# Seven block products for both down projections, with the weight sums made by adding DMA transfers

## The chip, the cores and the metric

One core of a Trainium2 chip runs the whole program in one launch. The time is that of the device, in microseconds (us): 1117.66 us is the median of three runs of the kernel before (1117.46 to 1119.12). Tokens are 512, the model is 1024 wide, the feed-forward layer 2816.

TensorE (PE in the profile) multiplies, VectorE (DVE), ScalarE (ACT) and GpSimd (POOL) do the work around it, and SyncE (SP) issues most transfers. Each engine runs its own instruction stream in order and waits on semaphores. The 16 DMA engines serve every queue.

## What is computed

Two transformer blocks, one after the other, all in float32. The parts that the change touches are the two feed-forward layers, and the norms behind them:

```
# first block                                   # second block
h = rms_norm(x, norm_ffn_pre)                   h2 = rmsnorm(x, norm2_g)
f = (silu(h @ w_gate) * (h @ w_up)) @ w_down    gate, up = h2 @ w_gate, h2 @ w_up
x = x + rms_norm(f, norm_ffn_post)              x = x + (silu(gate) * up) @ w_down
                                                return rmsnorm(x, final_g)
```

Ahead of each stand a norm, an input projection, attention and an output projection. In the first block attention is global for eight heads and windowed for eight, in the second it is causal with forget gates, beside pooled channels.

## The kernel before

**Precision.** A float32 operand is split in two fp32r parts, `high` (a rounded copy, made by ACT) and `low` (the rest, made by DVE), and a product is three matmuls: high by high, high by low, low by high.

**Weights.** They come as chunks of 512 KB (128 partitions by 8 tiles of 128 by 128). SP's `load(c)` puts chunk `c` in `raw`, a ring of four slots, once `vec_split` has read the chunk four before. `act_split` writes `wh` once the matmuls on the chunk four before are done (semaphore `used`), `vec_split` writes `wl`.

**Gate and up.** The first four of the 22 column tiles are multiplied plainly. The other 18 (`GROUPS`) are done by seven block products each (a two by two scheme of the Strassen kind, with 7 products of half size in place of 8), 7 products of 4 tiles by 256 tokens by 3 matmuls. One such group takes two chunks. DVE forms the sums of weight blocks that it needs (`vec_sum13`, `vec_s2`, `vec_s4`). The hidden values go to `gwhole`; `act_hidden_high` and `vec_hidden_low` split all 22 tiles to `gh` and `gl`.

**Down.** `pe_down` is plain: for each of 8 output tiles, 22 tiles of the hidden width, weights stationary, 512 tokens moving, 3 matmuls. The last output tile goes in two halves of 256 tokens, so that the norm behind it can begin on the first. Outputs stand with features on partitions. A chunk lasts PE for 8 tiles, since `DOWN` cuts the 22 tiles in 8, 8 and 6. In the first block `vec_down1` and `act_down1` square and sum the outputs, and the rest of the norm lies beside the first matmuls of `pe_in`, the second block's input projection. In the second block `vec_down2` adds x, `vec_final` multiplies by the norm's factor, and the output is stored.

**GpSimd.** It works in the first attention (`gpsimd_tick`), and then has nothing until the second (`gpsimd_attention2`). It issues no transfers.

## Time and profile before

| | us |
|---|---|
| median of 3 runs | 1117.66 |
| the profiled execution, its own span | 1115.9 |
| PE busy in it | 1092.9 (98%) |
| DVE busy | 832.3 (75%) |
| ACT busy | 612.6 (55%) |
| POOL busy | 121.2 (11%) |
| DMA: mean rate | 98 GB/s |

The span is that of one execution. Matmuls are pipelined, so a row's duration is longer than the distance from one matmul to the next; that distance, between the starts of two rows, is what a matmul costs. Stages by PE's rows: first down product 448.0 to 569.9 us, second 985.9 to 1107.75 us.

### The profile page before, as it was taken

To read this page: it belongs to the slowest core of one execution; us is meant where nothing else is said; L and a number is where in the kernel's file an instruction comes from. 1 tells how busy PE (TensorE), PEld (TensorE's weight loads), DVE (VectorE), ACT (ScalarE), POOL (GpSimd) and SP (SyncE) were. 2 spreads that over 40 slices of the span, in tenths; PEclk is the share of its full clock that TensorE was granted. 3 is DMA by queue.
4 is the path that set the end of the run, shared out by engine and by line. 5 is a ranking of instruction groups with operands and counts; after the bars stand their busy time and mean duration, and the time that the engine had idled before them with its cause. 6 is when DMAs were issued, how large, how long until landed. Compare 5 with 4: busy or idle time off the path is not lost.

```text
span 1115.9 us, 18197 instructions
## 1 busy us (share of the span) xinstructions
PE 1092.9 (98%) x6848; PEld 972.0 (87%) x6848; DVE 832.3 (75%) x1425; ACT 612.6 (55%) x1109; POOL 121.2 (11%) x143
## 2 busy tenths in 40 slices
PE   9999989999999999999999999999999999999997
PEld 6788877899999999888898887787899999988886
DVE  6898886798989888833378878566699898884333
ACT  6787785486555555522255558545555555563231
POOL 1476744000000000000000004200000000000000
PEclk9999999999999999999999999999999999999999
DMA  7323312312332333333313320031233233333312
GB/s 282 126 59 93 88 49 96 113 65 87 115 98 95 113 114 112 125 105 113 110 70 115 93 81 17 20 103 65 79 114 114 97 95 113 114 132 114 95 57 76
DMA packets 34150, 109.30 MB, mean 98 GB/s; under 512 B 4368, under 2 KB 7056, under 8 KB 33936
## 3 DMA queue, kind: packets, MB, share of 16 engines
q1 hardware_dynamic: 33312, 107.22, 29.5%
q8 instruction: 55, 0.90, 0.3%
q10 hardware_dynamic: 752, 0.92, 0.3%
q14 instruction: 31, 0.25, 0.1%
HBM read 100.78 MB, written 2.10 MB: 92 GB/s over the span
## 4 chain that ended last, share of the span: by engine, by line
PE 89%; DVE 5%; ACT 3%; issue 1%; DMA 1%; POOL 1%; ACTq 0%; SPq 0%; DVEq 0%
PE bank L551 13%; PE bank L553 13%; PE bank L552 13%; PE bank L2145 11%; PE bank L2144 11%; PE bank L2143 11%; PE bank L1086 2%; PE bank L1076 2%; PE bank L1031 1%; PE bank L1032 1%; PE bank L1033 1%; PE bank L1159 1%; PE bank L1160 1%; PE bank L1161 1%; PE bank L2630 1%
## 5 line engine op out<-in xcount | busy, mean ns | idle before, releaser
L472 DVE TENSOR_TENSOR wl<-raw,wh 128x1024 fp32r<-128x1024 f32 x108 | 134.0, 1242 | 132.0 <-ACT wh L460 131.6
L460 ACT ACTIVATE wh<-raw 128x1024 fp32r<-128x1024 f32 (+1 forms) x109 | 114.0, 1049 | 163.7 <-PE bank L553 152.8
L2143 PE MATMUL bank<-h,wh 128*128 128x256 f32 x576 | 163.0, 283 | 0.0
L2144 PE MATMUL bank<-h,wh 128*128 128x256 f32 x576 | 163.0, 283 | 0.0
L2145 PE MATMUL bank<-h,wl 128*128 128x256 f32 x576 | 163.0, 283 | 0.0
L2145 PE MATMUL bank<-hh,wl 128*128 128x256 f32 x432 | 122.3, 283 | 0.0
L2144 PE MATMUL bank<-hl,wh 128*128 128x256 f32 x432 | 122.3, 283 | 0.0
L2143 PE MATMUL bank<-hh,wh 128*128 128x256 f32 x432 | 122.2, 283 | 0.0
L551 PE MATMUL bank<-gh,wh 128*128 128x512 f32 x308 | 119.8, 389 | 0.0
L552 PE MATMUL bank<-gl,wh 128*128 128x512 f32 x308 | 119.8, 389 | 0.0
L553 PE MATMUL bank<-gh,wl 128*128 128x512 f32 x308 | 119.8, 389 | 0.0
L551 PE MATMUL bank<-hh,wh 128*128 128x512 f32 x288 | 116.2, 403 | 1.8 <-DVE wl L472 1.4
L552 PE MATMUL bank<-hl,wh 128*128 128x512 f32 x288 | 112.4, 390 | 0.0
L553 PE MATMUL bank<-hh,wl 128*128 128x512 f32 x288 | 112.3, 390 | 0.0
L2143 PEld LDWEIGHTS bank<-h,wh 128*128 128x128 f32 x576 | 110.6, 192 | 0.0
L2144 PEld LDWEIGHTS bank<-h,wh 128*128 128x128 f32 x576 | 110.6, 192 | 0.0
L2145 PEld LDWEIGHTS bank<-h,wl 128*128 128x128 f32 x576 | 110.6, 192 | 0.0
L2144 PEld LDWEIGHTS bank<-hl,wh 128*128 128x128 f32 x432 | 82.9, 192 | 0.1
L2143 PEld LDWEIGHTS bank<-hh,wh 128*128 128x128 f32 x432 | 82.9, 192 | 0.1
L2145 PEld LDWEIGHTS bank<-hh,wl 128*128 128x128 f32 x432 | 82.9, 192 | 0.0
L2297 ACT ACTIVATE wh<-raw 128x512 fp32r<-128x512 f32 (+1 forms) x72 | 60.4, 844 | 40.8 <-PE bank L2145 40.6
L2505 ACT ACTIVATE ta<-ta 128x256 f32<-128x256 f32 x72 | 29.8, 414 | 89.9 <-DVE ta L2324 89.9
(309 smaller groups left out, 2652.6 us busy)
## 6 DMA issues: line engine op xcount, KB each, us to landing
raw<-weights SPq DMA_DIRECT2D x181, 512.0 KB, 3.6
xres<-x_t SPq DMA_DIRECT2D x8, 512.0 KB, 6.2
sw<-ta SPq DMA_DIRECT2D x36, 64.0 KB, 2.0
out_t<-final SPq DMA_DIRECT2D x6, 256.0 KB, 2.1
q<-sw SPq DMA_DIRECT2D x10, 128.0 KB, 2.3
q<-ta SPq DMA_DIRECT2D x10, 128.0 KB, 2.3
rope<-angles SPq DMA_DIRECT2D x1, 1024.0 KB, 10.3
sw<-ta ACTq DMA_DIRECT2D x4, 64.0 KB, 2.8
```

The costliest lines, as they stand in the source:

```text
L460: act.activation(wh[:, j, :, n], raw[:, j, :, n], ACT.Copy).then_inc(high_split, 1)
L472: v.tensor_tensor(wl[:, j, :, :], raw[:, j, :, :], wh[:, j, :, :].bitcast(F32), ALU.subtract)\
L551: pe.matmul(bank[:, :], wh[:, slot, b, :], ah[:, k, :], start=first and n == 0, stop=False)
L552: pe.matmul(bank[:, :], wh[:, slot, b, :], al[:, k, :], start=False, stop=False)
L553: ins = pe.matmul(bank[:, :], wl[:, slot, b, :], ah[:, k, :], start=False, stop=last and n == len(blocks) - 1)
L1076: ins = pe.matmul(dst, a, b, start=i == 0, stop=i == len(todo) - 1)
L1086: ins = pe.transpose(bank[:, q * P:(q + 1) * P], pr1[:, s % PR1, q, kb * P:(kb + 1) * P], ident[:, :])
L2143: pe.matmul(o, wh_half[:, h, k, :], high[:, k, :], start=first and k == 0, stop=False, skip_group_check=True)
L2144: pe.matmul(o, wh_half[:, h, k, :], low[:, k, :], start=False, stop=False, skip_group_check=True)
L2145: ins = pe.matmul(o, wl_half[:, h, k, :], high[:, k, :], start=False, stop=k == HK - 1, skip_group_check=True)
L2297: act.activation(high, src, ACT.Copy).then_inc(gu.unit_high.of, 1)
L2505: act.activation(t, t, ACT.Silu).then_inc(gu.taken.of, 1)
```

## The change

Each down product is cut in two by two blocks: hidden halves of 11 tiles (`PAIR_TILES`), output halves of 512 columns, token halves `EARLY_TOKENS` and `LATE_TOKENS` of 256. Seven block products replace eight. In a product the tokens are now stationary (two blocks of 128) and 512 weight columns move, so the result has tokens on partitions. One product takes 11 tiles by 2 token blocks by 3 matmuls, and six chunks (`PER`), the sixth half empty.

- **Weight sums.** Four of the seven products need sums of weight blocks (S1 to S4). GpSimd makes them in device memory, by 8 transfers for each layer, each 768 rows of 4 KB (3.15 MB). Four copy a block, four add one to what is there (`accum_op`). Each waits for the one before. Both layers' 16 stand behind the first attention's work.
- **Token sums.** `gpsimd_token_sums` makes the sums of hidden values for the products P5, P6, P7 and P4 in batches of 4, 4 and 3 tiles. It stands on GpSimd behind all 16 transfers. `act_token_high` and `vec_token_low` split them in the down phase, one product ahead.
- **Taking the products.** `act_take` copies a product from PSUM to `ftok`, `vec_join` adds another. The order of products is P1, P2, P6, P5, P7, P3, P4.
- **Rows and features.** In the first block the normed rows are turned back by 32 transposes on PE (`pe_turn_rows`), 16 within the last product and 16 within `pe_in`. In the second, x is turned to rows by 32 transposes (`pe_turn_x`) within P6 and P5, and the output is stored by rows.
- **Gone.** `act_hidden_high` and `vec_hidden_low` (22 each for a layer), the sums on PE behind the down phases, the 512-wide reciprocals, `vec_scale` in the first block.

```diff
+SEVEN = (P1, P2, P6, P5, P7, P3, P4)
+BASE = {P1: W11, P2: W12, P4: W22}
+SUMMED = {P5: S1, P6: S2, P7: S3, P3: S4}
...
+        STEPS_SUMMED = {S1: 2, S2: 4, S4: 6, S3: 8}
+
+        def gpsimd_weight_sums(g, dn):
+            s = [dn.sums[i].rearrange("c p k n -> (c p) (k n)") for i in range(4)]
+            row = 4 * KB
+            g.dma_start(s[S1], blocks(dn, W21), max_dma_last_dim=row).then_inc(dn.sums_made, 16)
+            g.wait_ge(dn.sums_made, 16)
+            g.dma_start(s[S1], blocks(dn, W22), accum_op=ALU.add, max_dma_last_dim=row).then_inc(dn.sums_made, 16)
+            g.wait_ge(dn.sums_made, 32)
+            g.dma_start(s[S2], s[S1], max_dma_last_dim=row).then_inc(dn.sums_made, 16)
...
+        def gpsimd_token_sums(g, dn):
+            gu, sums, n = dn.gu, dn.token_sums, len(BATCHES)
+            early, late = EARLY_TOKENS, LATE_TOKENS
+            for batch in BATCHES:
+                t = ktiles(0, batch)
+                hidden_made(g, gu, t.stop - 1)
+                g.tensor_tensor(gwhole[:, t, early], gwhole[:, t, late], gwhole[:, t, early], ALU.subtract).then_inc(sums.of, 1)
+            reached(g, gu.product, 2 * GROUPS)
+            for i, batch in enumerate(BATCHES):
+                reached(g, sums, i + 1)
+                g.tensor_tensor(t2_whole[:, batch, :], gwhole[:, ktiles(1, batch), early], gwhole[:, ktiles(0, batch), early], ALU.add)\
+                    .then_inc(sums.of, 1)
...
+        def pe_block(pe, dn, x, chunk, row, b):
+            p, k, slot = SEVEN[x], 2 * chunk + row, (dn.c0 + PER * x + chunk) % RING
+            bank, n = down_pair(p)[b], slice(b * P, (b + 1) * P)
+            high, low = high_tokens[x % 2][:, k, n], low_tokens[x % 2][:, k, n]
+            pe.matmul(bank[:, :], high, wh_row[:, slot, row, :], start=k == 0 and p in (P1, P2, P5), stop=False, skip_group_check=True)
+            pe.matmul(bank[:, :], high, wl_row[:, slot, row, :], start=False, stop=False, skip_group_check=True)
+            return pe.matmul(bank[:, :], low, wh_row[:, slot, row, :], start=False, stop=k == PAIR_TILES - 1, skip_group_check=True)
...
+        def act_down_step(act, dn, x, n):
+            act_split(act, dn.c0 + PER * x + RING + n)
+            if x < 6 and n < len(BATCHES):
+                act_token_high(act, dn, x + 1, n)
...
@@ block.sync: load(c) @@
+                if down_chunk(c):
+                    name, x, i = down_chunk(c)
+                    p = SEVEN[x]
+                    if p in BASE:
+                        source = w_in[STORED0[name] + PER * BASE[p] + i]
+                    else:
+                        sp.wait_ge(downs[name].sums_made, 16 * STEPS_SUMMED[SUMMED[p]])
+                        source = downs[name].sums[SUMMED[p], i]
...
@@ block.gpsimd @@
             for t in range(TICK0, TICKS):
                 gpsimd_tick(g, t)
+            gpsimd_weight_sums(g, down1)
+            gpsimd_weight_sums(g, down2)
+            gpsimd_token_sums(g, down1)
             gpsimd_attention2(g)
+            gpsimd_token_sums(g, down2)
```

POOL, before, from the end of the first attention on (`sq`, `rh`: its last sums; `pr2`: the second attention's weights):

```order
L1475 TENSOR_TENSOR rh_69<-xres_57 128x512 [waits n_groupB_added,at1_added]
L1477 TENSOR_TENSOR sq_70<-sq_70,rh_69 128x512 [waits n_groupB_added,gpsimd_link]
L1930 TENSOR_SCALAR pr2_107<-pr2_107,rden_76 128x128 [waits at2_inverted]
L1930 TENSOR_SCALAR pr2_107<-pr2_107,rden_76 128x256 [waits at2_inverted]
```

Now, at the same place (the first layer's transfers, the turn to the second's, its last, and the token sums):

```order
L1494 TENSOR_TENSOR sq_70<-sq_70,rh_69 128x512 [waits n_groupB_added,gpsimd_link]
L2504 DMA down1_weight_sums<-weights 768x1024
L2506 DMA down1_weight_sums<-weights 768x1024 [waits down1_weight_sums]
L2508 DMA down1_weight_sums<-down1_weight_sums 768x1024 [waits down1_weight_sums]
...
L2518 DMA down1_weight_sums<-weights 768x1024 [waits down1_weight_sums]
L2504 DMA down2_weight_sums<-weights 768x1024 [waits down1_weight_sums]
...
L2518 DMA down2_weight_sums<-weights 768x1024 [waits down2_weight_sums]
L2546 TENSOR_TENSOR gwhole_83<-gwhole_83 128x4x256 [waits tiles_read,down2_weight_sums]
L2546 TENSOR_TENSOR gwhole_83<-gwhole_83 128x4x256 [waits gate_up_product]
L2546 TENSOR_TENSOR gwhole_83<-gwhole_83 128x3x256 [waits gate_up_product]
L2550 TENSOR_TENSOR t2_whole_90<-gwhole_83 128x1024 [waits down_token_sums,gate_up_product]
```

What stood directly behind the attention now has 16 transfers and twelve additions ahead of it; the first addition waits for the last transfer.

ACT, before, early in the first down phase (`wh<-raw`: weight splits; `sw<-bank`: the square of an output tile):

```order
L460 ACTIVATE wh_61<-raw_60 128x1024 [waits chunks_used,weights_loaded2]
L1937 ACTIVATE sw_66<-bank3 128x512 [waits chunks_used]
L460 ACTIVATE wh_61<-raw_60 128x1024 [waits chunks_used,weights_loaded3]
L460 ACTIVATE wh_61<-raw_60 128x1024 [waits chunks_used,weights_loaded0]
```

Now, in the second product of the first down phase (`high_tokens0<-t2_whole`: the tokens of P6, the third product):

```order
L2695 ACTIVATE ftok_91<-bank6 128x2x256 [waits chunks_used]
L2695 ACTIVATE ftok_91<-bank7 128x2x256
L491 ACTIVATE wh_61<-raw_60 128x1024 [waits chunks_used,weights_loaded2]
L2570 ACTIVATE high_tokens0_86<-t2_whole_90 128x1024 [waits chunks_used,down_token_sums]
L491 ACTIVATE wh_61<-raw_60 128x512 [waits chunks_used,weights_loaded3]
L2570 ACTIVATE high_tokens0_86<-t2_whole_90 128x1024 [waits chunks_used,down_token_sums]
```

Behind each of the first weight splits stands a split of tokens, which waits for GpSimd's sums; the weight splits behind it wait too.

## Rows read from the trace of the kernel before

**Rows 1.** The page: span, then busy time of each engine, share, instructions.

```profile
PE 1092.9 (98%) x6848; PEld 972.0 (87%) x6848; DVE 832.3 (75%) x1425; ACT 612.6 (55%) x1109; POOL 121.2 (11%) x143
```

**Rows 2.** The page: the chain that ended last, its share of the span.

```profile
PE 89%; DVE 5%; ACT 3%; issue 1%; DMA 1%; POOL 1%; ACTq 0%; SPq 0%; DVEq 0%
```

**Rows 3.** Timeline, first down product: start us, us, engine, line, operation, out<-in.

```profile
448.04 0.40 PE L551 MATMUL bank<-gh,wh 128*128 128x512 f32 x1
...
552.79 0.28 PE L2628 MATMUL bank<-gh,wh 128*128 128x256 f32 x1
...
569.90 0.28 PE L1176 MATMUL bank<-hh,wh 128*128 128x256 f32 x1
```

**Rows 4.** Timeline, second down product on PE: its first and last matmul.

```profile
985.90 0.40 PE L551 MATMUL bank<-gh,wh 128*128 128x512 f32 x1
...
1107.63 0.28 PE L2630 MATMUL bank<-gh,wl 128*128 128x256 f32 x1
```

**Rows 5.** Timeline, PE: four transposes (L675) between matmuls.

```profile
604.91 0.40 PE L553 MATMUL bank<-hh,wl 128*128 128x512 f32 x1
...
605.15 0.60 PE L675 MATMUL bank<-ident,ta 128*128 128x128 f32 x4
...
605.50 0.47 PE L560 MATMUL bank<-hh,wh 128*40 128x512 f32 x1
...
605.81 0.39 PE L561 MATMUL bank<-hl,wh 128*40 128x512 f32 x1
```

**Rows 6.** Timeline, PE: the sum (L620) within the input projection.

```profile
574.10 0.28 PE L1177 MATMUL bank<-hh,wl 128*128 128x256 f32 x1
...
574.46 0.47 PE L1176 MATMUL bank<-hh,wh 128*128 128x256 f32 x1
...
574.76 0.28 PE L1177 MATMUL bank<-hh,wl 128*128 128x256 f32 x1
```

**Rows 7.** Timeline, the program's end: [idle before <-releaser].

```profile
1107.95 0.42 DVE L2667 TENSOR_TENSOR xres<-xres,bank 128x256 f32<-128x256 f32 x1 [3.25 <-PE bank L2630]
...
1109.61 0.38 ACT L1702 ACTIVATE rstd<-bank 128x256 f32<-128x256 f32 x1 [0.39 <-PE bank L620]
...
1110.47 2.77 DVE L2675 TENSOR_TENSOR final<-final,rstd 128x256 f32<-128x256 f32 x8 [2.10 <-ACT rstd L1703]
...
1111.26 2.36 SPq L2730 DMA_DIRECT2D out_t<-final  x3
```

**Rows 8.** Timeline, POOL: its last piece in the first attention, its next one.

```profile
179.82 1.30 POOL L1477 TENSOR_TENSOR sq<-sq,rh 128x512 f32<-128x512 f32 x1
...
671.28 1.26 POOL L1930 TENSOR_SCALAR pr<-pr,rden 128x128 f32<-128x128 f32 x2 [490.16 <-DVE rden L1888]
```

**Rows 9.** Busy time by stretch: length; PE, PEld, DVE, ACT, POOL; PEclk, DMA share, GB/s.

```profile
8.00:22.00 14.00, 12.67 (x55) 9.85 (x55) 12.62 (x19) 11.77 (x22) 0.58 (x1) 1.00 0.91 367
...
182.00:448.00 266.00, 264.47 (x2028) 255.32 (x2027) 235.05 (x377) 153.40 (x263) 0.00 (x0) 1.00 0.33 106
...
448.00:553.00 105.00, 105.00 (x466) 87.00 (x465) 46.61 (x52) 33.32 (x41) 0.00 (x0) 1.00 0.34 112
...
1108.00:1116.00 8.00, 0.70 (x2) 0.30 (x2) 3.14 (x9) 1.61 (x4) 0.00 (x0) 0.83 0.37 131
```

**Rows 10.** The page, DMA issues: KB each, us to landing.

```profile
raw<-weights SPq DMA_DIRECT2D x181, 512.0 KB, 3.6
```

**Rows 11.** Instructions of line L1457, POOL: ns min/median/max, first and last start.

```profile
L1457 POOL TENSOR_TENSOR tb<-tb,sw x8: 1283/1690/2417, 44.5 to 142.5; 128x512 f32<-128x512 f32 x8
```

**Rows 12.** Groups by line within 448 to 553 us: xcount | busy us, mean ns | idle.

```profile
L472 DVE TENSOR_TENSOR wl<-raw,wh 128x1024 fp32r<-128x1024 f32 x22 | 26.9, 1224 | 56.5 <-ACT wh L460 56.4
...
L460 ACT ACTIVATE wh<-raw 128x1024 fp32r<-128x1024 f32 x22 | 23.3, 1058 | 68.4 <-PE bank L553 68.4
```

**Rows 13.** Timeline, one gate and up group: a load's issue and the weight sum.

```profile
381.67 20.49 SPq L2762 DMA_DIRECT2D raw<-weights  x5
...
388.11 1.22 DVE L2229 TENSOR_TENSOR first_sums<-raw 128x1024 f32<-128x1024 f32 x1
```

More of the change, by code:

```diff
@@ new lines, in gpsimd_token_sums @@
+        def gpsimd_token_sums(g, dn):
[10 more added lines that the diff above has]
+                    .then_inc(sums.of, 1)
+            for k_half in range(2):
+                for i, batch in enumerate(BATCHES):
+                    t = ktiles(k_half, batch)
+                    reached(g, sums, n + i + 1)
+                    reached(g, dn.token_low, n * k_half + i + 1)
+                    g.tensor_tensor(gwhole[:, t, late], t2_whole[:, batch, :], gwhole[:, t, late], ALU.subtract).then_inc(sums.of, 1)
@@ new lines, in chunk_rows, with pe_chunk_ready, pe_chunk @@
+        def chunk_rows(chunk):
+            return range(1 if chunk == PER - 1 else 2)
+        def pe_chunk_ready(pe, dn, x, chunk):
+            slot_wait(pe, dn.c0 + PER * x + chunk)
+            if chunk % 2 == 0:
+                reached(pe, dn.token_low, len(BATCHES) * x + chunk // 2 + 1)
+        def pe_chunk(pe, dn, x, chunk):
+            pe_chunk_ready(pe, dn, x, chunk)
+            for row in chunk_rows(chunk):
+                for b in range(2):
+                    ins = pe_block(pe, dn, x, chunk, row, b)
+            ins.then_inc(used, 1)
@@ new lines, in pe_down1, with rows_of @@
+        def pe_down1(pe):
+            for x in range(7):
+                chain_free(pe, down1, SEVEN[x])
+                if x == 1:
+                    pe_factor(pe, down1)
+                for chunk in range(PER):
+                    if x == 6 and chunk == 3:
+                        pe_turn_rows(pe, 0, (0, 1))
+                    if x == 6 and chunk == 4:
+                        pe_turn_rows(pe, 0, (2, 3))
+                    pe_chunk(pe, down1, x, chunk)
+        def rows_of(b, d):
+            return ftok[:, 4 * (b % 2) + 2 * d:4 * (b % 2) + 2 * d + 2, b // 2, :]
@@ new lines, in act_take, with vec_join @@
+        def act_take(act, dn, p, b, d):
+            act.wait_ge(used, multiplied(dn, SEVEN.index(p) + 1, 0))
+            for i in range(2):
+                act.activation(rows_of(b + i, d), as_rows(down_pair(p)[i][:, :]), ACT.Copy).then_inc(dn.taken.of, 1)
+        def vec_join(v, dn, p, b, d):
+            v.wait_ge(used, multiplied(dn, SEVEN.index(p) + 1, 0))
+            reached(v, dn.taken, {P2: 2, P7: 6, P3: 6}[p])
+            for i in range(2):
+                o = rows_of(b + i, d)
+                v.tensor_tensor(o, o, as_rows(down_pair(p)[i][:, :]), ALU.add).then_inc(dn.joined.of, 1)
@@ L2726, in store @@
-        def store(eng, half, k, tiles):
-            n = HALVES[half]
-            eng.wait_ge(x_final, KT * half + k + tiles)
-            eng.dma_start(out[:, k:k + tiles, n], final[:, k:k + tiles, n]).then_inc(out_stored, 16)
+            vec_gain(v, 3, 0)
+            reached(v, first_block, 1)
+            vec_x(v, 2, 1, as_rows(PAIR_B[0][:, :]))
+            vec_x_mean(v, 1)
+            vec_final(v, 2)
+            v.wait_ge(used, multiplied(down2, 7, 0))
+            vec_x(v, 3, 1, as_rows(PAIR_B[1][:, :]))
@@ L2778, in _ @@
                 load(c)
-            for k in range(0, KT, 2):
-                store(sp, 0, k, 2)
-            store(sp, 1, 0, 2)
-            store(sp, 1, 4, 2)
-            store(sp, 1, 7, 1)
-            sp.wait_ge(out_stored, 16 * 9)
+            for b in range(3):
+                store(sp, b, slice(0, D), 2 * b + 2)
+            store(sp, 3, slice(D // 2, D), 7)
+            sp.wait_ge(out_stored, 16 * 5)
         @block.gpsimd
```

758 lines of the change are left out of this document (462 added, 296 removed).

## The prediction

> **What bounds the kernel now.** I read the page's busy times first: PE is busy in 98% of the span [rows 1]. Then the chain of work that ended last, to see that this is work that is waited for and not only overlapping rows: 89% of it is PE [rows 2]. Then the timeline of both down phases. The first runs from 448.04 to 569.90 us, the second from 985.90 to the end of its last matmul at 1107.75, each 121.9 us without a gap [rows 3, 4]. What takes matmuls out there shortens the program, as long as nothing new makes PE wait. Last I read GpSimd and the DMA engines, because the change gives them work: GpSimd ends its part of the first attention at 181.1 us and then has nothing until 671.3 [rows 8]; the DMA engines are 33% busy from 182 to 448 us, moving 106 GB/s [rows 9]. The measured time, 1117.66, is 1.8 us above the span of the profiled execution, 1115.9; I sum on the span's rows and add the sum to 1117.66.
>
> **Down products on PE.** Seven output tiles of 22 hidden tiles and 3 matmuls are 462 matmuls of 512 columns, from 448.04 to 552.79: 104.75 us, 0.227 each [rows 3]. The seven block products are 7 x 11 x 2 x 3 = 462 matmuls of the same shape, so 104.75 us again; that the stationary side is now tokens changes nothing in the shape. What goes is the eighth tile with its sums, 552.79 to 569.90: 17.1 us for each layer. What comes:
> - Transposes. Four take 0.35 us (605.15 to 605.50), and the matmul behind them 0.31 where others take 0.23: 0.43 for four [rows 5]. Four such sets lie in the first down phase (1.7), four in the input projection (1.7), eight in the second down phase (3.4).
> - Four matmuls of one column to turn the factor, in each phase. No row has one; between 0.1 and 0.6 us, I take 0.3.
> - In the input projection a sum goes: 0.36 and 0.30 between starts where 0.12 each is usual, 0.4 [rows 6].
>
> First layer: -17.1 + 1.7 + 0.3 + 1.7 - 0.4 = -13.8. Second: -17.1 + 3.4 + 0.3 = -13.4. The program's end now lasts 8.2 us behind the last matmul: a subtraction, square, sum, two ACT steps of 0.4, eight multiplications in 2.77, and the stores [rows 7]. Afterwards there are an addition, a square beside a multiplication, two small ACT steps, one multiplication and one store. I take -1.1, with -2.5 and +1 as ends. Together **-28.3**, so 1089.4 if nothing waits.
>
> **Splits in the down phase.** Chunks now last PE 12 x 0.227 = 2.72 us in place of 5.45. In a product's 15.0 us DVE has 5.5 weight splits of 1.22 and tokens worth 2.75 of them, 10.1 us, plus at most two additions of 0.7; ACT has 8.25 of 1.06, 8.7 us, plus two copies [rows 12]. Both fit. A slot freed by PE is needed again 8.2 us later and takes 1.06 + 1.22 plus a token split of each, 4.6. The loads need 2.9 MB in 15.0 us, 192 GB/s. That is above the 112 of this phase now, but the engines moved 367 GB/s at 0.91 share early in the program [rows 9]. I cost this at nothing; if the cover is gone, DVE's 4 us of slack in a product are what is used up first. The splits of 22 hidden tiles that go lay beside PE's work and give nothing back.
>
> **The chain of transfers.** GpSimd issues the 16 transfers one at a time, each waiting for the one before, from 181.1 us. Then come the token sums. Who waits for them is ACT, at its first split of the tokens of P6, and behind that stands the weight split of the last chunk of the second product. PE comes to that chunk at 448 + 15.0 + 5 x 2.72 = 476.6 us. From the chain's end E to that chunk there are: three additions for P5 (1024, 1024 and 768 columns; 512 take 1.29 us undisturbed, so 6.9 [rows 11]), one for P6 (2.5), ACT's token split 1.06, DVE's 1.22, and half a weight split on each, of which about 1.0 is in series: 12.7. So PE loses E - 463.9 us, if that is above zero. Later products wait no more, since GpSimd makes a batch in 2.5 us and PE takes 5.4 over it.
>
> So E decides, and no row shows a transfer from memory to memory, or one that adds. I bound them by loads. At full share the engines move 367 / 0.91 = 403 GB/s [rows 9]; 3.15 MB make one pass in 7.8 us. Beside the loads of gate and up (106 of 403) it is 7.8 / 0.74 = 10.5. What a transfer costs besides: a load of 512 KB lands in 3.6 us [rows 10], of which 1.3 are the pass, so 2.3. A copy takes one pass if its write lies wholly beside its read, two if they share what limits them. An addition has two reads and a write: two passes or three.
> - Low end, 1 and 2: (10.5 + 21.0 + 4.6) x 8 = 289 us, E about 477, loss 13.
> - High end, 2 and 3: (21.0 + 31.5 + 4.6) x 8 = 457 us of this rate. By 448, 267 are done; to 476.6, beside 192 GB/s of loads, about 21 more; then PE stands, nothing is loaded, and the remaining 169 shrink to 0.77, 130. E is 607, the loss 143.
> - Taken, 1.5 and 2.5: 46.8 x 8 = 374. 267 and 21 done by 476.6, 86 left, 66 us alone. E = 543, **the loss 79**. I take the middle, since read and write go to the same memory here, where a load writes elsewhere; no row is nearer to one end.
>
> Below the low end there is little room: all 16 in one pass would end at 386, but an addition must read twice. Behind a stand of that length PE starts again at a lower clock. Where it idles, at the program's end, the granted clock of the stretch is 0.83 in place of 1.00 [rows 9]: part of it was at the lower level. I add 2 us.
>
> Sum: 1117.66 - 28.3 + 79 + 2 = **1170.4**.
>
> The Trainium skill (DMA: Bandwidth & Descriptors, Latency and other measured facts) gives copies between HBM tensors a full rate of 214 GB/s, an estimate of 14.7 us for 3.15 MB alone, near two of my passes. With that for the copies the chain would be 33 us longer at its own rate, and the loss about 104. No row here shows it.
>
> **Rivals.**
> 1. *The chain is hidden or nearly.* The loss is under 28.3 when E is under 492, that is when a copy and an addition together take less than about 38.5 us beside loads. One pass and two passes, 36.1, do; then the time is 1102, and with a slightly better rate (E under 464) 1089. For it: 67% of the DMA share is free [rows 9], and nothing else of GpSimd waits. Against: every byte is read from and written to the memory that also feeds the loads, and each of 16 completions is waited for. Chance 0.24, of which half is at 1089.
> 2. *Copies at two passes, additions at four.* (21.0 + 42.0 + 4.6) x 8 = 541; 253 left at 476.6 become 195, E is 671, the loss 208, the time 1299. It is what a copy at half a load's rate, and an addition at half a copy's, would do. The Trainium skill (Collectives: The Full Stack, on the bandwidth ceiling) has that last ratio: adding there runs at half the rate of copying, because of two source reads. Chance 0.08.
> 3. *The transfers hold up gate and up.* A load issued at 381.67 lands 3.7 us later, and DVE adds from it at 388.11 [rows 10, 13]: 2.7 us in hand. If the chain makes a load land later than 6.4 us, each of the 18 groups grows; by 1 us each, 18 us. But then the chain starts no later and the down phase starts later, so with a late chain this is swallowed by the same wait, and with a hidden one the time is 1107. I give it 0.1, within the other cases.
> 4. *The change doesn't do what it says:* PE's count of matmuls is plain from the code, so I give this nothing.
>
> **How the numbers follow.** Late chain beyond the break-even, 1118 to 1250: 0.66, the likeliest, by itself 1120 to 1240. Rival 2: 0.08. Rival 1: 0.24. The rest, 0.02, is a chain that just eats the gain. A measurement of this kernel tells 0.2%, 2.2 us, from no change. So faster 0.24, same 0.02, slower 0.74. The range reaches from the hidden case to the high end with some of rival 3: 1089 to 1250.
>
> **What would show it.** Right: GpSimd's first token addition starts near 543 us, PE idles once, for 60 to 140 us, in the first down phase at the second product's last chunk, released through ACT's token split by GpSimd; the second down phase takes 108.5 us without a gap; DMA share above 0.9 from 181 us on. Wrong: GpSimd adds tokens before 464 us; or PE's idle time is spread over the gate and up groups; or a second gap stands in the down phases, behind loads or DVE. If the copies take much more or less than 18 us and the additions than 29, the mechanism is right and its size is not.

## The result, and the profile after

The changed kernel takes 1155.2 us (median of 4 runs, 1150.1 to 1161.7), the kernel before 1117.9 (4 runs beside them); the ratio is 1.0337, 95% interval 1.0301 to 1.0372. Forecast were 1170.4, 1089 to 1250, and slower with a chance of 0.74. The profiled execution spans 1159.9 us and is the slowest of its four, so the stages below add up to 44.0 us more than before, where the medians differ by 37.4.

The stages go from one first matmul to the next, in us, read from PE's timeline (the last one ends with the start of its last matmul); differences are of the unrounded times:

| stage | before | after | difference | forecast |
|---|---|---|---|---|
| to the first layer's group phase | 266.6 | 266.7 | 0.1 | 0 |
| groups of gate and up, first layer | 181.4 | 205.1 | +23.7 | 0 |
| first down phase | 121.9 | 137.9 | +16.0 | -15.1, +79, +2 |
| projection, attention and the rest, to the second layer's groups | 234.6 | 239.3 | +4.8 | +1.3 |
| groups, second layer | 181.4 | 184.1 | +2.6 | 0 |
| second down phase | 121.7 | 120.2 | -1.5 | -13.4 |
| end | 8.2 | 6.6 | -1.7 | -1.1 |

The page of the changed kernel, first the busy time of each engine (us, share, instructions) and the slices of the span, then the added queue (packets, MB, share of 16 engines) and the chain that ended last. It answers to [rows 1, 2]: PE is busy for 9.4 us less than before, and 93% instead of 98%; 27% of the chain is DMA.

```profile
span 1159.9 us, 18071 instructions
## 1 busy us (share of the span) xinstructions
PE 1083.5 (93%) x6648; PEld 954.5 (82%) x6648; DVE 896.8 (77%) x1428; ACT 661.9 (57%) x1177; POOL 201.2 (17%) x183
...
PE   8999999999998899938998999999999999998997
...
PEclk9999999999999999977999999999999999998999
DMA  7422317998898898944651421004223333334653
...
q0 software_dynamic: 12544, 50.33, 17.6%
...
PE 52%; DMA 27%; DVE 9%; ACT 5%; issue 4%; POOL 3%; ACTq 0%; SPq 0%; DVEq 0%; POOLq 0%
```

GpSimd's timeline of the changed kernel (start, us, engine, line, operation, [idle before <-releaser]): the transfers, cut to the first four and the last two, and the token sums behind them. Before, this engine stood idle here [rows 8]. A copy is followed by the next issue 13.8 to 18.6 us later, an addition by 23.7 to 26.6; the sixteen take 326.9 us.

```profile
181.12 0.92 POOL L2504 DMA_DIRECT2D down_weight_sums<-weights  x1
196.82 1.18 POOL L2506 DMA_DIRECT2D down_weight_sums<-weights  x1 [14.78 <-DMA down_weight_sums<-weights]
223.42 0.71 POOL L2508 DMA_DIRECT2D down_weight_sums<-down_weight_sums  x1 [25.42 <-DMA down_weight_sums<-weights]
237.67 1.14 POOL L2510 DMA_DIRECT2D down_weight_sums<-weights  x1 [13.54 <-DMA down_weight_sums<-down_weight_sums]
...
465.83 0.70 POOL L2516 DMA_DIRECT2D down_weight_sums<-weights  x1 [23.02 <-DMA down_weight_sums<-weights]
481.92 1.15 POOL L2518 DMA_DIRECT2D down_weight_sums<-weights  x1 [15.38 <-DMA down_weight_sums<-weights]
508.04 6.39 POOL L2546 TENSOR_TENSOR gwhole<-gwhole 128x1024 f32<-128x1024 f32 x3 [24.98 <-DMA down_weight_sums<-weights]
514.40 7.39 POOL L2550 TENSOR_TENSOR t_whole<-gwhole 128x1024 f32<-128x1024 f32 x3
521.76 18.07 POOL L2557 TENSOR_TENSOR gwhole<-t_whole,gwhole 128x1024 f32<-128x1024 f32 x6
```

PE's and ACT's timelines of the changed kernel, and one row of DVE's: the stall of the first down phase, the waits of the second, and one in each layer's last group (the second layer's shown). They answer to [rows 3, 4], where PE had no gap. For the wait of 3.75 us the profile names no releaser (`issue`); DVE's split of that chunk, the last row, ends at 528.98, just ahead of it.

```profile
516.76 1.06 ACT L2570 ACTIVATE high_tokens<-t_whole 128x1024 fp32r<-128x1024 f32 x1 [24.50 <-POOL t_whole L2550]
...
522.40 0.80 PE L2609 MATMUL bank<-wh,high_tokens 128*128 128x512 f32 x1 [20.54 <-DVE wl L504]
529.08 0.77 PE L2609 MATMUL bank<-wh,high_tokens 128*128 128x512 f32 x1 [3.75 <-issue]
...
1030.11 0.39 PE L2070 MATMUL bank<-hh,wh 128*128 128x256 f32 x1 [2.39 <-ACT acc L2392]
1048.83 0.50 PE L2609 MATMUL bank<-wh,high_tokens 128*128 128x512 f32 x1 [1.96 <-DVE wl L504]
1054.89 0.79 PE L2609 MATMUL bank<-wh,high_tokens 128*128 128x512 f32 x1 [2.18 <-DVE wl L504]
1061.25 0.50 PE L2609 MATMUL bank<-wh,high_tokens 128*128 128x512 f32 x1 [1.12 <-DVE wl L504]
...
525.61 3.37 DVE L504 TENSOR_TENSOR wl<-raw,wh 128x1024 fp32r<-128x1024 f32 x1
```

So there are four costs, not one: the stall, longer groups, waits for DVE's splits, and small waits from the order of ACT and DVE. In the groups it is the loads. DMA issues between 182 and 440 us, of the kernel before and then of the changed one (KB each, median us from issue to landing): a load lands 9.1 us after its issue in place of 3.6 [rows 10, 13 showed single ones], and 2.7 us were in hand.

```profile
raw<-weights SPq DMA_DIRECT2D x47, 512.0 KB, 3.6
```

```profile
down_weight_sums<-weights POOLq DMA_DIRECT2D x9, 3072.0 KB, 23.4
raw<-weights SPq DMA_DIRECT2D x43, 512.0 KB, 9.1
down_weight_sums<-down_weight_sums POOLq DMA_DIRECT2D x4, 3072.0 KB, 14.6
```

### The profile page after: what moved, and what is told of

It reads as the page before. It is cut to its first block, busy times and chain, and to the rows that moved or that the text cites. A ratio compares the mean times of both kernels' runs of the same rounds, so it can differ in the third digit from the quotient of the medians.

```text
span 1159.9 us, 18071 instructions
## 1 busy us (share of the span) xinstructions
PE 1083.5 (93%) x6648; PEld 954.5 (82%) x6648; DVE 896.8 (77%) x1428; ACT 661.9 (57%) x1177; POOL 201.2 (17%) x183
## 4 chain that ended last, share of the span: by engine, by line
PE 52%; DMA 27%; DVE 9%; ACT 5%; issue 4%; POOL 3%; ACTq 0%; SPq 0%; DVEq 0%; POOLq 0%
DMA down_weight_sums<-weights 21%; PE bank L583 6%; PE bank L584 6%; PE bank L585 6%; DMA down_weight_sums<-down_weight_sums 5%; PE bank L2072 5%; PE bank L2071 5%; PE bank L2070 5%; PE bank L2609 4%; PE bank L2611 4%; PE bank L2610 4%; DVE wl L504 3%; PE bank L1093 2%; PE bank L1103 1%; ACT wh L491 1%
## 5 line engine op out<-in xcount | busy, mean ns | idle before, releaser
L504 DVE TENSOR_TENSOR wl<-raw,wh 128x1024 fp32r<-128x1024 f32 (+1 forms) x144 | 191.1, 1334 | 76.4 <-ACT wh L491 75.0
L491 ACT ACTIVATE wh<-raw 128x1024 fp32r<-128x1024 f32 (+1 forms) x145 | 145.5, 1008 | 130.1 <-PE bank L2611 59.5
L2070 PE MATMUL bank<-h,wh 128*128 128x256 f32 x576 | 165.9, 288 | 13.1 <-ACT rh L2386 13.1
L2071 PE MATMUL bank<-h,wh 128*128 128x256 f32 x576 | 165.0, 286 | 0.0
L2609 PE MATMUL bank<-wh,high_tokens 128*128 128x512 f32 x308 | 125.1, 406 | 31.0 <-DVE wl L504 27.3
L2070 PEld LDWEIGHTS bank<-h,wh 128*128 128x128 f32 x576 | 112.3, 195 | 14.7 <-ACT rh L2386 14.7
L2610 PE MATMUL bank<-wl,high_tokens 128*128 128x512 f32 x308 | 122.8, 399 | 0.0
L2611 PE MATMUL bank<-wh,low_tokens 128*128 128x512 f32 x308 | 122.4, 398 | 0.0
L2071 PEld LDWEIGHTS bank<-h,wh 128*128 128x128 f32 x576 | 112.6, 196 | 0.0
L2609 PEld LDWEIGHTS bank<-wh,high_tokens 128*128 128x128 f32 x308 | 59.3, 193 | 46.9 <-DVE wl L504 30.7
```

Of the source, the lines that this page charges most:

```text
L491: act.activation(wh[:, j, b, n], raw[:, j, b, n], ACT.Copy).then_inc(high_split, 1)
L504: v.tensor_tensor(wl[:, j, b, :], raw[:, j, b, :], wh[:, j, b, :].bitcast(F32), ALU.subtract)\
L2070: pe.matmul(o, wh_half[:, h, k, :], high[:, k, :], start=first and k == 0, stop=False, skip_group_check=True)
L2071: pe.matmul(o, wh_half[:, h, k, :], low[:, k, :], start=False, stop=False, skip_group_check=True)
L2609: pe.matmul(bank[:, :], high, wh_row[:, slot, row, :], start=k == 0 and p in (P1, P2, P5), stop=False, skip_group_check=True)
L2610: pe.matmul(bank[:, :], high, wl_row[:, slot, row, :], start=False, stop=False, skip_group_check=True)
```

## The experiments

Theory A: the transfers cost, by their end (GpSimd's token sums wait for it) and by their traffic (loads land late). Theory B: GpSimd's token sums hold up DVE's splits. Rival C: the down phases' own loads, 192 GB/s, starve PE whatever else is done. Theory D: waits made by the order of ACT's and DVE's work, with a lower granted clock behind them. Theory E: how long a load is held up depends on the transfers' packets. Stages are named as in the table above; all of them, for every kernel:

| kernel | us | ratio to before, 95% | to groups | groups 1 | down 1 | between | groups 2 | down 2 |
|---|---|---|---|---|---|---|---|---|
| before | 1118 | | 266.6 | 181.4 | 121.9 | 234.6 | 181.4 | 121.7 |
| changed | 1155.2 | 1.034 (1.030, 1.037) | 266.7 | 205.1 | 137.9 | 239.3 | 184.1 | 120.2 |
| e1 no weight sums | 1122.9 | 1.004 (1.003, 1.006) | 266.2 | 185.6 | 117.3 | 240.9 | 185.5 | 118.9 |
| e2 second layer later | 1159.8 | 1.038 (1.036, 1.039) | 268.1 | 198.4 | 142.3 | 238.4 | 184.1 | 120.2 |
| e3 copies only | 1144.4 | 1.024 (1.022, 1.027) | 266.6 | 206.1 | 117.2 | 240.9 | 185.5 | 118.9 |
| e4 no sums at all | 1105.0 | 0.989 (0.987, 0.990) | 266.6 | 185.6 | 107.5 | 240.6 | 184.1 | 110.5 |
| e5 placed | 1147.9 | 1.026 (1.024, 1.028) | 294.0 | 184.1 | 117.2 | 240.8 | 184.1 | 120.2 |
| e6 placed, paced | 1131.2 | 1.012 (1.010, 1.013) | 292.3 | 185.3 | 107.8 | 240.9 | 185.5 | 111.5 |
| e7 placed, ordered | 1147.4 | 1.026 (1.024, 1.028) | 293.9 | 184.2 | 117.3 | 236.7 | 185.4 | 120.8 |
| e8 all three | 1124.7 | 1.007 (1.004, 1.009) | 292.0 | 184.2 | 107.5 | 236.7 | 185.4 | 111.7 |
| e9 first in the groups | 1108.2 | 0.990 (0.989, 0.992) | 268.6 | 190.7 | 109.5 | 236.7 | 181.5 | 113.6 |
| e10 packets of 1 KB | 1123.1 | 1.004 (1.002, 1.006) | 266.8 | 194.2 | 109.4 | 246.8 | 181.5 | 113.5 |
| e11 packets of 8 KB | 1121.5 | 1.001 (1.000, 1.003) | 275.9 | 196.2 | 109.5 | 236.7 | 181.5 | 113.5 |
| e12 first sums later | 1109.1 | 0.992 (0.991, 0.993) | 266.4 | 190.2 | 109.8 | 236.7 | 181.5 | 115.0 |

### e1: no weight sums

```diff
-            gpsimd_weight_sums(g, down1)
-            gpsimd_weight_sums(g, down2)
...
-                        sp.wait_ge(downs[name].sums_made, 16 * STEPS_SUMMED[SUMMED[p]])
-                        source = downs[name].sums[SUMMED[p], i]
+                        source = w_in[STORED0[name] + PER * SUMMED[p] + i]
```

> All 16 transfers are left out, with the weight sums that they make: the four sum products load blocks of w_down in their place, the same bytes in the same order, and nothing waits for sums. Theory A (the transfers' end sets GpSimd's token sums, and their traffic delays the loads of the first gate and up groups): those groups fall from 205.1 us back to 181.4, and the 20.5 us gap in the first down phase is gone. Theory B (GpSimd's token sums slow DVE's splits): the second down phase stays near 120 us and the first comes down from 137.9 to about the same 120, with DVE's 128x1024 subtractions at 2.8 to 3.4 us while GpSimd adds. A and B together: 1155.2 - 23.7 - 18 - about 3 in the input projection, some 1110 to 1113. Rival C (the down phases' own loads, 192 GB/s, are what starves them): gaps behind loads stay and the time is 1125 or more. If B is wrong and the transfers did all of it: about 1092 to 1098.

Measured 1122.9. Theory A holds: the groups lose 19.5 of their 23.7 us, and the stall is gone. But I expected 1110 to 1113: without any transfer the change still costs 5 us where it should give 28. The groups stay 4 us above 181.4, the projection 6 us, and the down phases take 117 and 119 us.

### e4: no token sums either

```diff
-            gpsimd_token_sums(g, down1)
...
-            gpsimd_token_sums(g, down2)
...
-                reached(act, dn.token_sums, len(BATCHES) * (P5, P6, P7, P4).index(p) + i + 1)
+                reached(act, dn.gu.product, 2 * GROUPS)
...
-                return t2_whole[:, batch, :]
+                return gwhole[:, ktiles(0, batch), EARLY_TOKENS]
```

> As the run without weight sums, and GpSimd's token sums are left out too: the products read unsummed tokens and the splits wait for no sum. What is left of the change is PE's order, the splits and the loads. Theory B: DVE's splits of 128x1024 take 1.22 us throughout, both down phases last 108.5 to 111 us, and the time is 18 to 24 us below that of the run without weight sums, about 1089 to 1093. Rival (the splits' order and slots make PE wait, whatever GpSimd does, or the loads do): the down phases stay near 120 us and the two runs differ by under 4 us.

The run is 17.9 us below e1, and nearly all of it lies in the down phases, which are 9.8 and 8.4 us shorter: 107.5 and 110.5 us, near the 106.8 and 108.5 of the forecast's sum. This is theory B. DVE's timeline of the second down phase in e1, beside GpSimd's nine sums (start, us, line, operation):

```profile
1000.77 3.42 DVE L504 TENSOR_TENSOR wl<-raw,wh 128x1024 fp32r<-128x1024 f32 x1
1004.11 2.87 DVE L2583 TENSOR_TENSOR low_tokens<-gwhole,high_tokens 128x1024 fp32r<-128x1024 f32 x1
1006.91 2.89 DVE L504 TENSOR_TENSOR wl<-raw,wh 128x512 fp32r<-128x512 f32 x1
```

and at the same place in e4, without them:

```profile
990.42 1.23 DVE L504 TENSOR_TENSOR wl<-raw,wh 128x1024 fp32r<-128x1024 f32 x1 [1.15 <-ACT wh L491]
991.56 1.22 DVE L2583 TENSOR_TENSOR low_tokens<-gwhole,high_tokens 128x1024 fp32r<-128x1024 f32 x1
992.70 0.69 DVE L504 TENSOR_TENSOR wl<-raw,wh 128x512 fp32r<-128x512 f32 x1
```

The half-size split takes 2.89 in place of 0.69: DVE is not slower, it waits. Rival C falls: with the same down loads and nothing else, the longest gap of PE in both down phases is 0.7 us. Its 1105.0 is still above the 1089 to 1093 that I expected, by the groups and the projection (4.1, 2.6 and 4.7 us), and by 2.7 us in the down phases that no run explains. The first part is theory D's, and here it can be read. Stretches of e4's first layer, around the wait of 2.39 us at 447.7 us (length; PE, PEld, DVE, ACT, POOL; granted clock, DMA share, GB/s):

```profile
440.00:448.00 8.00, 5.61 (x46) 5.41 (x45) 5.18 (x9) 5.80 (x10) 0.00 (x0) 0.99 0.40 131
448.00:456.00 8.00, 8.00 (x41) 7.35 (x41) 6.88 (x10) 3.63 (x5) 0.00 (x0) 0.80 0.36 100
```

Behind a stand of 2.4 us the granted clock of the next 8 us is 0.80, part of it at the lower level: 1.6 us more. In the second layer of the same execution the same wait has 1.00 behind it, and that phase is 1.5 us shorter (184.1 against 185.6). So the clock's part comes in some executions and not in others.

### e2: the second layer's transfers behind the token sums

```diff
-            gpsimd_weight_sums(g, down2)
             gpsimd_token_sums(g, down1)
+            gpsimd_weight_sums(g, down2)
```

> The complete kernel; the second layer's eight transfers come behind the first down phase's token sums in place of ahead of them. Theory A: the first chain ends near 345 us, GpSimd's first token sum stands near 448 or earlier, no gap of 20 us in the first down phase. The gate and up groups run beside transfers for 164 of their 267 us only, so their excess of 23.7 us falls to about 14. The second chain then runs from about 480 to 660 us, beside the down loads, the input projection and the start of the second attention. If only waiting for the chain's end costs: 1155.2 - 18 - 9 = 1128. If its traffic delays the down loads (192 GB/s) as it delays those of the groups, the first down phase keeps 5 to 15 us of it: 1133 to 1143. Rival C (loads starve the down phase whatever the order): no shorter than 1150.

Measured 1159.8, no gain, where theory A gave 1128 to 1143. It fits the 1150 or more of rival C, which e4 rules out. The stall did go, and the groups fell by 6.7 us, as theory A says. But the eight transfers that were moved now run beside the down loads, and there they cost 25.0 us (142.3 against 117.3), where I had allowed 5 to 15. Between 495 and 600 us the DMA share is 0.98, a load lands in 10.3 us, and PE stands eight times for 1.1 to 2.7 us. The loads of e1 between 480 and 585 us land in 4.1. First e2, then e1:

```profile
raw<-down_weight_sums SPq DMA_DIRECT2D x20, 512.0 KB, 10.3
raw<-weights SPq DMA_DIRECT2D x9, 512.0 KB, 7.9
```

```profile
raw<-weights SPq DMA_DIRECT2D x33, 512.0 KB, 4.1
```

### e3: copies in place of additions

```diff
-            g.dma_start(s[S1], blocks(dn, W22), accum_op=ALU.add, max_dma_last_dim=row).then_inc(dn.sums_made, 16)
+            g.dma_start(s[S1], blocks(dn, W22), max_dma_last_dim=row).then_inc(dn.sums_made, 16)
```

(and so for the other three additions of a layer)

> The eight adding transfers copy in place of adding, so what they leave out is the additions; their number, order and waits stay. In the trace of the changed kernel a copy is waited for 13 to 18 us, an addition 22.6 to 25.4. If an addition costs its second read, the 16 take 16 x 14 to 17 = 225 to 270 us, end at 410 to 450 us, GpSimd's token sums start by 450 and the 20.5 us gap goes. The first gate and up groups: if it is any traffic at a share of 0.9 that delays the loads (theory A), they stay near 200 us, since copies fill the same window; if it is adding itself, with the engines held longer for each packet, they fall to 190 or below. Time 1127 to 1142.

The sixteen copies end at 428 us, 15.4 us each. The first down phase then takes 117.2 us, the same as without any transfer: a chain that ends ahead of the group phase's end does not stall PE, and the 20.5 us were its end and nothing else. The groups stay at 206.1: any traffic at this share delays the loads (8.6 us to landing), adding or not. 1144.4 lies 2 us above my range.

### e5: the transfers placed where no weight stream is pressed

```diff
+            gpsimd_weight_sums(g, down1, (0,))
             for t in range(TICK0, TICKS):
                 gpsimd_tick(g, t)
-            gpsimd_weight_sums(g, down1)
-            gpsimd_weight_sums(g, down2)
+                if t in SUMS_AT:
+                    gpsimd_weight_sums(g, down1, (SUMS_AT.index(t) + 1,))
             gpsimd_token_sums(g, down1)
+            g.wait_ge(used, multiplied(down1, 7, 0))
+            gpsimd_weight_sums(g, down2, range(6))
             gpsimd_attention2(g)
```

(SUMS_AT is 2, 12, 19, 29, 36, 49, 58; of the second layer's last two, one stands in the second attention, one behind it)

> The complete kernel; only the time at which GpSimd issues the 16 transfers moves. The first layer's eight are issued one by one through the first attention (the first at 25 us, the last at about 161), the second layer's from the end of the first down phase's last product on (about 560 to 720 us, the last one behind the second attention). If traffic beside the loads of gate, up and down is what costs (theory A), nothing of it is left there: the first groups take the 185.6 us that they take without any transfer, the first down phase 117, and the time is that of the run without weight sums, 1122.9, plus at most 4 for small transfers of the first attention and the input projection that land later: 1123 to 1127. Rival: the attention and the projection wait for their own small transfers as the groups waited for theirs; then the 32 us saved come back there and the time stays above 1140.

Half right. Behind the first down phase eight transfers cost nothing: 240.8 us against 240.9 without. In the first attention eight cost 27 us, and the rival holds there. Its small transfers (64 KB, a rotation's swap) land in 6.3 us in place of 2.0, and GpSimd waits 19.1 us for them in place of 5.0, against only 2.0 for the transfers that it issued itself. Between 30 and 182 us the DMA share is 0.76 in place of 0.27, and PE's granted clock 0.91 in place of 1.00. How the 27 us divide between the waits and the clock is not shown. Issues between 30 and 182 us, e5 and then e1:

```profile
sw<-ta SPq DMA_DIRECT2D x32, 64.0 KB, 6.3
```

```profile
sw<-ta SPq DMA_DIRECT2D x32, 64.0 KB, 2.0
```

### e6: token sums paced

```diff
                 reached(g, sums, i + 1)
+                g.wait_ge(used, multiplied(dn, 0, (1, 3, 5)[i]))
...
                     reached(g, dn.token_low, n * k_half + i + 1)
+                    g.wait_ge(used, multiplied(dn, *((1, 3), (1, 5), (2, 3), (2, 5), (3, 4), (4, 4))[n * k_half + i]))
```

> As the run before it, and GpSimd's token sums for P6, P7 and P4 are held back by waits on PE's finished chunks, so that one stands in each third to half of a product and not nine in a row. The sum of GpSimd's work is the same. Without any token sum the time was 17.9 us lower. Theory B (what costs is a backlog: 26.5 us without a break in which a DVE subtraction takes 2.8 to 3.4 us instead of 1.22, while DVE has some 10 of 15 us of work): spread out, DVE's slack takes it and 12 to 17 us of the 17.9 come back: 1107 to 1112. Rival (each GpSimd sum costs PE its share whenever it runs): no more than 4 us come back.

16.7 us of the 17.9 come back, with the same nine sums of GpSimd: the down phases take 107.8 and 111.5 us. What cost was the backlog, as theory B says. (The 1107 to 1112 us named were counted from the time that e5 had been expected to reach.)

### e7 and e8: the order

```diff
-            for n in range(len(BATCHES)):
-                act_token_high(act, dn, 0, n)
-            act_split(act, d0 + 1)
+            act_token_high(act, dn, 0, 0)
             act_c5(act, gu, m)
+            act_token_high(act, dn, 0, 1)
+            act_token_high(act, dn, 0, 2)
+            act_split(act, d0 + 1)
...
-            pe_turn_rows(pe, 1, (0, 1))
             pe_high_half(pe, ph.c0, 0, ph.h, [(k, j) for k in (6, 7) for j in range(3)])
+            pe_turn_rows(pe, 1, (0, 1))
...
-            vec_split(v, i0 + 3)
             vec_row_mean(v, 1)
             vec_scale_rows(v, 1)
+            vec_split(v, i0 + 3)
```

> As the run with the transfers placed elsewhere, with three changes of order. In the last gate and up group ACT takes PE's product of P5 out of its bank behind one token split in place of three and a weight split. In the input projection PE does the first tiles' products with blocks 6 and 7 ahead of the transposes of the second half's rows, and DVE makes the mean and the scaling ahead of its split of the fourth chunk. Theory D: PE's waits of 2.39 us in both layers and of 2.48 in the projection go, each with the stretch of lower granted clock (0.80 to 0.83 in the 8 us behind it, 1.4 to 1.6 us more): 6 to 8 us for the groups and 3 to 4 for the projection, together 9 to 12 less. Rival: the wait was slack of the group and comes back one product later, and the clock dips for another reason; then under 4 us less.

The projection gives 4.1 us, about the 3 to 4 expected; the groups give none. The wait of 2.39 us only moved one product on, where DVE frees the bank behind its split of the next down chunk, which now came later:

```profile
1014.82 0.58 PE L2072 MATMUL bank<-h,wh 128*128 128x256 f32 x1 [2.52 <-DVE sw L2252]
```

So here the rival held, and the whole gives 0.5 us, within the spread.

> All of it together: transfers placed, token sums paced, order changed. If the three causes are separate and add up: 1123 to 1127, less 12 to 17, less 9 to 12, that is 1096 to 1105, faster than the kernel before (1118) and the best of all of them. If pacing and order remove the same waits, or the paced sums stand in the way of the last group, it is no better than the better of the two single ones.

Pacing and the projection's order add up (23.2 us less than e5), but the first attention's 27 us and the moved wait keep it at 1124.7.

### e9: a kernel faster than both

On e8, the first layer's transfers go back behind the first attention, and DVE frees that bank first:

```diff
-            gpsimd_weight_sums(g, down1, (0,))
...
+            gpsimd_weight_sums(g, down1, range(8))
             gpsimd_token_sums(g, down1)
...
+            vec_c22(v, gu, m)
             vec_split(v, d0 + 1)
-            vec_c22(v, gu, m)
```

> The complete kernel. The first layer's transfers go back to where the change has them (behind the first attention, eight of them, over by about 341 us); the second layer's stay behind the first down phase, where they cost nothing (595.0 to 836.0 us took 241.0 with them, 240.9 without). Token sums paced. The order as in the run before, and DVE now frees the bank of P7 ahead of its split of the second down chunk too, since the wait of 2.39 us at P5 had only moved there (2.5 us, released by DVE). By the sum of the parts: the run without any sums 1105.0; the first layer's traffic beside the groups + 12.8; order in the projection - 4.2; the wait of 2.4 to 2.5 us in both layers with its clock - 5 to -8; left over of the token sums + 0 to 2: 1106 to 1111, 0.6 to 1.1% faster than the kernel before. If traffic in the first attention was as cheap as in the groups (that is, the 27 us there came from something else than the transfers), it stays above 1118.

1108.2 us, 0.96% faster than before (0.83% to 1.08%), within what was expected. The second layer's groups take 181.5 us, as in the kernel before: both waits are gone. But half of what the second layer's groups gain (185.4 to 181.5) comes back behind them: its down phase takes 113.6 us, in e8 111.7, and the first one 109.5 and 107.5. Each has a wait of 1.0 us that e8 has not. The first layer's groups take 190.7, for the eight transfers beside them.

### e10 and e11: the size of the packets

```diff
-            row = 4 * KB
+            row = KB
```

> As the run before it, with rows of 1 KB in place of 4 KB in the 16 transfers. Theory E (a load's packets stand in the engines behind the transfers' 4 KB packets, turn by turn; shorter ones let it pass sooner): loads in 182 to 340 us land in less than the 9.1 us of the changed kernel, the excess of the groups, about 13 us, falls by half or more, the chain takes longer, and the time is 5 to 8 us below the run before. Rival (the memory's bandwidth is what they share, or each packet costs a fixed time): the excess stays or grows, since the transfers last longer: 0 to 15 us above it.

> As the run with the first layer's transfers beside the groups (1108.2), with rows of up to 8 KB in place of 4 KB in all 16 transfers. With rows of 1 KB a load landed sooner (7.3 us in the median of 182 to 340 us, against 8.9), but the additions took 26.8 us against 22.9 and the groups gained nothing. If a load waits behind packets in the engines (theory E), it lands later now, 10 us or more, and the groups' excess of 9.2 us over 181.46 grows by 2 to 5 us unless the additions fall below 21 us. If every packet costs a fixed time on top of its bytes, the additions and copies get shorter, 19 to 21 and 12 to 13 us, and the excess shrinks to 6 to 8. If rows are not made longer than 4 KB at all, packets and time are as before, 1108.

(the second with 8 * KB.) The edit did not do all that it was meant to: in e10's trace only the additions have packets of 1 KB (3072 each), and the copies keep 768 of 4 KB; in e11 both have 384 of 8 KB. Theory E is right in its direction: loads between 182 and 340 us land in 7.3 us in e10, 8.9 with 4 KB, 9.6 with 8 KB. It buys nothing. The first layer's four additions land in 27.0 us (median) in e10, 24.3 in e9 and 21.6 in e11; the 26.8, 22.9 and 21.5 of the expectation are the profile's medians over additions and copies from `weights` together. The groups exceed 181.5 us by 12.8 (e10) and 14.8 (e11), where e9 has 9.2: e10 was expected 5 to 8 us below e9 and is 15 above, and why the groups of e11 are longest although its transfers are shortest is open. In e10 they also reach into the second attention, where GpSimd then waits for one and PE for GpSimd (4.9 and 4.0 us). With 8 KB ACT waits 11.6 us for one weight load in the first output projection, and PE 6.6 behind it. Both are slower than e9. These two scatter more than the others (1115.9 to 1126.6 and 1115.2 to 1124.2), so only their sign is to be trusted.

### e12: the first sums later

```diff
-                g.wait_ge(used, multiplied(dn, 0, (1, 3, 5)[i]))
+                g.wait_ge(used, multiplied(dn, 0, (3, 5, PER + 1)[i]))
```

> As the run with the first layer's transfers beside the groups (1108.2), with GpSimd's three token sums of P6 held back until PE has done 3 and 5 chunks of the first product and 1 of the second, in place of 1, 3 and 5. In that run PE still waits 1.0 us in both layers at the fourth down chunk, released by DVE's split of it, which took about 3.2 us beside the first of these sums (two splits 6.46 us). Theory B: both waits go, and with them what the granted clock costs behind them: 2 to 5 us less, 1103 to 1106. Rival (the third sum now comes too late for the split of P6's last tokens, or the backlog only moves): no gain, up to 3 us more.

No gain: the wait of 1.0 us stays in both layers, and the trace says why. GpSimd's and DVE's timelines of e12:

```profile
993.07 2.41 POOL L2546 TENSOR_TENSOR t_whole<-gwhole 128x1024 f32<-128x1024 f32 x1 [110.64 <-PE bank L2608]
...
993.13 3.43 DVE L504 TENSOR_TENSOR wl<-raw,wh 128x1024 fp32r<-128x1024 f32 x1 [1.15 <-ACT wh L491]
996.48 1.21 DVE L2580 TENSOR_TENSOR low_tokens<-gwhole,high_tokens 128x1024 fp32r<-128x1024 f32 x1
...
996.62 0.50 PE L2606 MATMUL bank<-wh,high_tokens 128*128 128x512 f32 x1 [1.00 <-DVE wl L504]
```

The third finished chunk, to which I had moved the first sum, falls 0.06 us ahead of the very split that PE waits for. It is also the cleanest picture of the mechanism: GpSimd's sum ends at 995.48, and DVE's split, begun at 993.13, ends 1.08 us after that, about its own 1.22. Both read and write SBUF, the core's memory for tiles. The Trainium skill (SBUF — State Buffer, SBUF: two separate sides) says that a DVE instruction with two inputs in SBUF and a GpSimd instruction that reads SBUF exclude each other for the whole instruction; this row agrees.

The trace of the kernel before has the same picture, in the first attention (GpSimd's rows, then DVE's):

```profile
43.01 1.30 POOL L1453 TENSOR_TENSOR sw<-sw,rope 128x512 f32<-128x512 f32 x1 [2.49 <-DMA sw<-ta]
46.62 1.30 POOL L1463 TENSOR_TENSOR tb<-tb,hsq 128x512 f32<-128x512 f32 x1
...
43.61 1.78 DVE L472 TENSOR_TENSOR wl<-raw,wh 128x1024 fp32r<-128x1024 f32 x1
47.13 1.88 DVE L472 TENSOR_TENSOR wl<-raw,wh 128x1024 fp32r<-128x1024 f32 x1
```

The splits end 1.08 and 1.09 us after GpSimd's addition. There DVE's subtraction with one input in PSUM, where PE's products land (L1219, 128x512), takes 0.67 to 0.69 us in all 16 cases beside such an addition, as it does alone.

Back to back, both pay: GpSimd's sum takes 3.0 us (18.07 for six) in place of 2.41.

## Why the prediction was right, and where it was not

The sign, its main cause and the chain of who waits for whom were right; the total came out near by two errors that partly cancel.

1. *Matmuls.* Right. Where almost nothing waits (e4), the down phases last 107.5 and 110.5 us; the sum had 106.8 and 108.5, 2.7 less. The end gave 1.7 us, 1.1 were taken.
2. *The length of the chain.* Mechanism right, size off. A pair of copy and addition was taken at 46.8 us; it took 40.9 (326.9 / 8). A copy took 16.1 us from issue to issue (18 taken), an addition 24.8 (29 taken). So E was 508.0, not 543. The Trainium skill's rate for such copies, 214 GB/s (DMA: Bandwidth & Descriptors, Latency and other measured facts), an estimate of 14.7 us alone, would have put the loss at 104; copies took 16.1 us beside 96 GB/s of other traffic, nearly all of it loads (24.64 MB in the 258 us from 182 on), less than my own term. The Trainium skill's ratio of two between adding and copying (Collectives: The Full Stack, The bandwidth ceiling) was 1.54 here.
3. *The loss, E - 463.9.* Right as a rule. PE came to the waiting chunk 23.7 us later than assumed, because the groups had grown, and so the loss in the down phase should be 508.0 - 487.6 = 20.4; measured 20.54. That it fits to 0.1 us is luck: PE came another 1.6 us later, held up in the first two products, and the way from the chain's end to PE took 14.4 us in place of 12.7, because DVE's splits stood beside GpSimd's sums. Together with the groups the loss is 44, not 79, and 4.2 of it are in the groups without any transfer (e1). Rival 3 is what happened ("with a late chain this is swallowed by the same wait"), with 23.7 us in place of 18: of the 44 us that a stall alone would have cost, 23.7 were spent ahead of it.
4. *Splits in the down phase, "I cost this at nothing".* This step failed. DVE's 10.1 of 15.0 us counted each split at 1.22, its time beside an idle GpSimd [rows 12]. Beside GpSimd's sums it is 2.8 to 3.4. The second down phase is 11.8 us longer than the sum and the first, without its stall, 10.6; without GpSimd's sums (e4) 9.7 and 9.9 us of these are gone. Part is waits for DVE and part the lower clock that comes with them. In the second, the waits above 0.5 us are 6.0 us, and a granted clock of 0.96 over the 120 us is worth about 5 (an estimate). In the first, 4.5 us are waits behind the stall, and the clock is 0.67 from 522.4 to 540 us, at most 5.8 us, where I had taken 2. I gave GpSimd's sums a duration and looked who waits for them, not whom they hold up.
5. *Order at the seams.* Not in the sum: 2.6 us in the second groups and 3.5 in the projection (+4.8, less the 1.3 that were counted). ACT's three token splits stood ahead of the copy that frees P5's bank, and PE's transposes ahead of work that needed nothing.

Steps 4 and 5 are some 28 us, the whole of what the removed matmuls give. So the rival with a hidden chain, 1089 to 1102, could not have come out as the code stood: e1, which has no chain at all, takes 1122.9. Of the chances the 0.24 for "faster" was therefore too high. Of the signs named, the gap "at the second product's last chunk, released through ACT's token split by GpSimd" was there, with 20.5 us and not 60 to 140, and the DMA share was 0.90 from 182 to 440 us. But "the second down phase takes 108.5 us without a gap" was not so, and two signs of being wrong were there: "PE's idle time is spread over the gate and up groups" (nine waits above 0.5 us, 15.9 us together) and "a second gap stands in the down phases, behind loads or DVE". The trace of the kernel before could have warned of the latter. Rows 11 give a GpSimd addition 1.28 to 2.42 us, of which I took the shortest as undisturbed, and two of DVE's splits took 1.78 and 1.88 us there (shown under e12).

Not settled: why 8 transfers beside the groups cost 12.8 us (e2 against e1) in the complete order and 9.2 in e9. Where the 6.5 us between the profiled execution and the median went can't be read from one trace.

## What to carry to other kernels

A background transfer is not free because the mean DMA share is low: ask, for each stretch that it runs through, how many microseconds a load there may be late. Here eight such transfers cost 0, 9 to 13, 25 or 27 us by where they ran. Work given to an idle GpSimd needs a second question beside its own end, whose instructions it excludes; if it does, spread it, since the neighbour's slack takes single collisions but not nine in a row.

## What the runs showed of the hardware

- From memory to memory, 3 MB by GpSimd's queue took 13.8 to 18.6 us as a copy and 23.7 to 26.6 as an addition, beside 96 GB/s of other traffic. On average adding costs 1.54 copies (24.8 and 16.1 us).
- At a DMA share of 0.90 a load of 512 KB lands in 9.1 us instead of 3.6 at 0.32, and at 0.76 a transfer of 64 KB in 6.3 instead of 2.0 at 0.27. With background packets of 4 and 8 KB the load takes 8.9 and 9.6 us, and 7.3 with additions of 1 KB packets between copies of 4 KB.
- A DVE subtraction of two SBUF tensors and a GpSimd addition hardly overlap: 1.22 and 2.41 us alone, 3.43 for the DVE one when it comes 0.06 us behind. With one input in PSUM a DVE subtraction keeps its 0.69 us.
- PE's stand of 2.4 us was followed by 8 us at a granted clock of 0.80 in one layer and of 1.00 in the other layer of the same execution.
